# One 512-column product for the high and low activations in the residual's dense layers and in the second block's gate and up

## What is computed

```python
x = x + gate_f * ((jax.nn.silu(u_gate) * u_val) @ w_down[l])            # first block: down
...
for layer in range(DEPTH_2):
    h = h + hybrid_mixer(...)                    # ends in y @ w_mix_out: mixout0, mixout1
    h = h + memory_cross_attention(...)          # ends in o @ w_xo:      xo0, xo1
    hn = rmsnorm(h, norm_ffn_g[layer])
    if layer % 2 == 0:
        h = h + (jax.nn.silu(hn @ w_gate) * (hn @ w_up)) @ w_down       # up2, down2
    else:
        h = h + moe_swiglu(...)
```

## Time and profile before

| | |
|---|---|
| median of 3 executions | 2247.67 us (2243.60 to 2249.77) |
| the profiled execution | 2247.01 us, span 2245.3 us |
| TensorE matmul, busy | 2183.2 us, 97% of the span |
| VectorE busy | 1701.4 us, 76% |
| ScalarE busy | 1296.6 us, 58% |
| DMA | 563.82 MB, mean 251 GB/s |
| granted TensorE clock, mean | 0.990 |

### The profile page before, as it was taken

How to read it: one execution, slowest core, us unless ns; L and a number is a source line. 1 busy time by engine, 2 the same in 40 slices (tenths; PEclk the granted TensorE clock), 3 DMA queues, 4 the chain that set the end, 5 groups by cost and what they waited for, 6 DMA issues and landing times.

```text
span 2245.3 us, 34129 instructions
## 1 busy us (share of the span) xinstructions
PE 2183.2 (97%) x13631; PEld 1948.4 (87%) x13631; DVE 1701.4 (76%) x1889; ACT 1296.6 (58%) x1289; POOL 76.1 (3%) x159
## 2 busy tenths in 40 slices
PE   7999999999999999999999999999999999999997
PEld 5989988999989899999898888888887888888886
DVE  6768967884785465558654888888888888888887
ACT  3564434763425444443344777777777777777775
POOL 5002200000000000000000000000000000000000
PEclk9999999999999999999999999999999999999999
DMA  9746858655635366555372799999999999999995
GB/s 287 193 127 217 269 175 236 175 173 178 175 116 173 104 170 177 181 155 156 116 239 81 268 365 361 369 329 365 359 369 350 321 370 362 364 345 358 365 365 184
DMA packets 414601, 563.82 MB, mean 251 GB/s; under 512 B 17098, under 2 KB 268212, under 8 KB 414448
## 3 DMA queue, kind: packets, MB, share of 16 engines
q1 hardware_dynamic: 409680, 555.26, 73.5%
q0 software_dynamic: 4768, 6.36, 1.2%
HBM read 559.75 MB, written 1.84 MB: 250 GB/s over the span
## 4 chain that ended last, share of the span: by engine, by line
PE 83%; DVE 8%; ACT 2%; issue 1%; DVEq 0%; ACTq 0%
PE pair L1174 59%; PE misc L1174 13%; PE pair L1234 4%; DVE wlo L1808 2%; DVE opf L1876 2%; PE misc L1717 1%; DVE wlo L2157 1%; PE pair L1685 1%; ACT whi L674 1%; PE misc L1274 1%; PE misc L1253 0%; DVE hl L1827 0%; PE misc L1694 0%; PE misc L1695 0%; PE misc L1365 0%
## 5 line engine op out<-in xcount | busy, mean ns | idle before, releaser
L2157 DVE TENSOR_TENSOR wlo<-raw,whi 128x2048 fp32r<-128x2048 f32 x336 | 764.2, 2290 | 119.6 <-ACT whi L1056 118.9
L1056 ACT CAST whi<-raw 128x2048 fp32r<-128x2048 f32 x336 | 643.1, 1917 | 205.0 <-PE pair L1174 123.5
L1808 DVE TENSOR_TENSOR wlo<-raw,whi 128x2048 fp32r<-128x2048 f32 (+2 forms) x158 | 348.5, 2209 | 157.9 <-ACT whi L674 157.2
L1174 PE MATMUL pair<-hh,whi 128*128 128x256 f32 x1408 | 405.5, 288 | 8.4 <-DVE opl L1827 4.1
L1174 PE MATMUL pair<-hl,whi 128*128 128x256 f32 x1408 | 400.7, 285 | 0.0
L1174 PE MATMUL pair<-hh,wlo 128*128 128x256 f32 x1408 | 400.4, 284 | 0.0
L1174 PE MATMUL pair<-whi,oph 128*128 128x512 f32 x896 | 353.5, 395 | 5.2 <-issue 4.5
L1174 PE MATMUL pair<-wlo,oph 128*128 128x512 f32 x896 | 350.0, 391 | 0.0
L1174 PE MATMUL pair<-whi,opl 128*128 128x512 f32 x896 | 349.7, 390 | 0.0
L674 ACT CAST whi<-raw 128x2048 fp32r<-128x2048 f32 (+2 forms) x158 | 290.1, 1837 | 84.7 <-PE pair L1174 66.8
L1174 PE MATMUL pair<-oph,whi 128*128 128x256 f32 x976 | 279.4, 286 | 5.2 <-issue 3.0
(11 more groups left out here) (464 smaller groups left out, 2788.1 us busy)
## 6 DMA issues: line engine op xcount, KB each, us to landing
raw<-in_moe_w_gate_dram SPq DMA_DIRECT2D x112, 1024.0 KB, 7.1
raw<-in_moe_w_up_dram SPq DMA_DIRECT2D x112, 1024.0 KB, 7.3
raw<-in_moe_w_down_dram SPq DMA_DIRECT2D x112, 1024.0 KB, 7.0
raw<-in_w_in_dram SPq DMA_DIRECT2D x38, 1024.0 KB, 6.1
raw<-in_w_mod_dram SPq DMA_DIRECT2D x24, 1024.0 KB, 5.7
raw<-in_w_up_dram SPq DMA_DIRECT2D x44, 512.0 KB, 5.2
raw<-in_w_xkv_dram SPq DMA_DIRECT2D x16, 1024.0 KB, 5.7
raw<-in_ffn_w_gate_dram SPq DMA_DIRECT2D x22, 512.0 KB, 4.1
```

Source lines behind the costliest of these rows:

```text
L1056: act.copy(whi[:, q, :], raw[:, r, :]).then_inc(sem("hi_ready"), 1)
L1174: ins = pe.matmul(out_, lhs, rhs, start=start and i == 0, stop=stop and i == 2)
L1808: dve.tensor_tensor(wlo[:, i_ % SPLIT, 0:size], raw[:, raw_of(n), 0:size], whi[:, i_ % SPLIT, 0:size].bitcast(F32), ALU.subtract).then_inc ...
L2157: dve.tensor_tensor(wlo[:, q, :], raw[:, r, :], whi[:, q, :].bitcast(F32), ALU.subtract).then_inc(sem("lo_ready"), 1)
```

## The change

For six stages, listed in `TWO_SUMS`, the two products with the same high weights become one matmul. `hh` and `hl` (and `oph` and `opl`) are now two halves of one tensor `hx` (`opx`), so that a chunk's high and low part can be the moving operand together: 2 x 256 = 512 columns, in two runs. It fills a whole PSUM bank: high x high in columns 0 to 255, high x low in columns 256 to 511. The product of the low weights is added to the first half. The readers now add the second half as well.

```diff
+TWO_SUMS = ("down", "mixout0", "mixout1", "xo0", "up2", "down2")
...
-        hh = sb("hh", [P, DC, T], F32R)
-        hl = sb("hl", [P, DC, T], F32R)
+        hx = sb("hx", [P, 2, DC, T], F32R)
+        hh, hl = hx[:, 0], hx[:, 1]
...
+        up_sum = aview(3072, 3, 2, T)
...
+                            if groups[ups2[j]][0] in TWO_SUMS:
+                                act.wait_ge(sem("slot_used"), split_no[first_slot[ups2[j]]] + 1)
+                                act.copy(up_sum[:, j % 3], pair[:, pair_seq[ups2[j]] % PAIRS, :, T:2 * T]).then_inc(sem("up2_second"), 1)
                             act.wait_ge(sem("up2_gate"), j + 1)
                             act.activation(sg[:, j % 3], gate_n[:, j % 3], ACT.Silu).then_inc(sem("up2_silu"), 1)
...
+            def both(out_, w_hi, w_lo, x, start, stop):
+
+                pe.matmul(out_.rearrange("p (k t) -> p k t", k=2), w_hi, x, start=start, stop=False)
+                return pe.matmul(out_[:, 0:T], w_lo, x[:, 0], start=False, stop=stop)
...
-                            ins = three(pair[:, q, m, 0:T], wh[:, col], wl[:, col], operand(xh, x), operand(xl, x), start, stop)
+                            parts = operand(x_parts, x)
+                            if groups[g][0] in TWO_SUMS:
+                                ins = both(pair[:, q, m, :], wh[:, col], wl[:, col], parts, start, stop)
+                            else:
+                                ins = three(pair[:, q, m, 0:T], wh[:, col], wl[:, col], parts[:, 0], parts[:, 1], start, stop)
...
+            def second(g):
+
+                return pair[:, pair_seq[g] % PAIRS, :, T:2 * T]
+
             def add_modulated(g, j, gate):
                 ps = group(g)
+                if groups[g][0] in TWO_SUMS:
+                    for m in range(2):
+                        t = 2 * j + m
+                        ins = dve.scalar_tensor_tensor(xT[:, t], second(g)[:, m], mod[:, gate + t:gate + t + 1], xT[:, t], ALU.mult, ALU.add)
+                    link(ins)
...
             def add_plain(g, j):
                 ps = group(g)
+                if groups[g][0] in TWO_SUMS:
+                    link(dve.tensor_tensor(xT[:, 2 * j:2 * j + 2, :], second(g), xT[:, 2 * j:2 * j + 2, :], ALU.add))
                 dve.tensor_tensor(xT[:, 2 * j:2 * j + 2, :], ps, xT[:, 2 * j:2 * j + 2, :], ALU.add).then_inc(sem("dve_read"), 1)
...
-                            dve.tensor_tensor(gate_n[:, j % 3], ps[:, 0], rt[:], ALU.mult).then_inc(sem("up2_gate"), 1)
+                            if groups[ups2[j]][0] in TWO_SUMS:
+                                dve.wait_ge(sem("up2_second"), j + 1)
+                                both = up_sum[:, j % 3]
+                                link(dve.tensor_tensor(both, ps, both, ALU.add))
+                            else:
+                                both = ps
+                            dve.tensor_tensor(gate_n[:, j % 3], both[:, 0], rt[:], ALU.mult).then_inc(sem("up2_gate"), 1)
...
-                            dve.tensor_tensor(uf[:, j % 3], ps[:, 1], sg[:, j % 3], ALU.mult).then_inc(sem("dve_read"), 1)
+                            dve.tensor_tensor(uf[:, j % 3], both[:, 1], sg[:, j % 3], ALU.mult).then_inc(sem("dve_read"), 1)
                     for j, g in enumerate(stage_groups["down2"]):
                         ps = group(g)
-                        link(dve.tensor_tensor(down_n, ps, rt[:].unsqueeze(1).to_broadcast([P, 2, T]), ALU.mult))
+                        by_token = rt[:].unsqueeze(1).to_broadcast([P, 2, T])
+                        link(dve.tensor_tensor(down_n, second(g), by_token, ALU.mult))
+                        link(dve.tensor_tensor(xT[:, 2 * j:2 * j + 2, :], down_n, xT[:, 2 * j:2 * j + 2, :], ALU.add))
+                        link(dve.tensor_tensor(down_n, ps, by_token, ALU.mult))
                         dve.tensor_tensor(xT[:, 2 * j:2 * j + 2, :], down_n, xT[:, 2 * j:2 * j + 2, :], ALU.add)\
                             .then_inc(sem("dve_read"), 1)
```

More of the change, by code:

```diff
@@ L402, in build_program, with up2_parts @@
         fin = [b[:, 16:24, :] for b in (oph, opl)]
+        xin_at, fin_at = opx[:, :, 0:8, :], opx[:, :, 16:24, :]
+        up_sum = aview(3072, 3, 2, T)
+        def up2_parts(j):
+            return opx[:, :, j] if j < 16 else hx[:, :, j - 16]
         def up2_out(k, j):
-            return (oph, opl)[k][:, j] if j < 16 else (hh, hl)[k][:, j - 16]
+            return up2_parts(j)[:, k]
         values_at = [b[:, 16:24, :].rearrange("p a b -> p (a b)").rearrange("p (i d) -> p i d", i=TB) for b in (oph, opl)]
@@ L1187, in free_pair, with dense_group @@
                     pe.wait_ge(sem(f"{groups[before][2]}_read"), reads_at[before])
+            def both(out_, w_hi, w_lo, x, start, stop):
+                pe.matmul(out_.rearrange("p (k t) -> p k t", k=2), w_hi, x, start=start, stop=False)
+                return pe.matmul(out_[:, 0:T], w_lo, x[:, 0], start=False, stop=stop)
             def operand(x, c):
-                return x(c) if callable(x) else x[:, c]
-            def dense_group(g, xh, xl, weights_move=False, width=256, chunk0=0, each_chunk=None):
+                return x(c) if callable(x) else x[:, :, c]
+            def dense_group(g, x_parts, weights_move=False, width=256, chunk0=0, each_chunk=None):
                 free_pair(g)
@@ L1213, in dense_group @@
                             tok = slice(m * P, (m + 1) * P)
-                            ins = three(pair[:, q, m, 0:width], wh[:, 0:width], wl[:, 0:width], xh[:, x, tok],
-                                        xl[:, x, tok], start, stop, True)
+                            ins = three(pair[:, q, m, 0:width], wh[:, 0:width], wl[:, 0:width], x_parts[:, 0, x, tok],
+                                        x_parts[:, 1, x, tok], start, stop, True)
                         else:
                             col = slice(m * P, (m + 1) * P)
-                            ins = three(pair[:, q, m, 0:T], wh[:, col], wl[:, col], operand(xh, x), operand(xl, x), start, stop)
+                            parts = operand(x_parts, x)
[3 more added lines that the diff above has]
+                                ins = three(pair[:, q, m, 0:T], wh[:, col], wl[:, col], parts[:, 0], parts[:, 1], start, stop)
                     ins.then_inc(sem("slot_used"), 1)
@@ L1276, in sums, with into_norm @@
                     ins.then_inc(sem("squares_summed"), 1)
-            def into_norm(stage, name, xh, xl, beside=None, **how):
+            def into_norm(stage, name, x_parts, beside=None, **how):
                 each = how.pop("each_chunk", None)
                 for j, g in enumerate(stage_groups[stage]):
-                    dense_group(g, xh, xl, each_chunk=each if j == 0 else None, **how)
+                    dense_group(g, x_parts, each_chunk=each if j == 0 else None, **how)
                     if j >= 1:
@@ L1375, in _ @@
                     qk_squares(i - 1)
-            dense_group(stage_groups["va"][0], hh, hl, weights_move=True, width=P)
+            dense_group(stage_groups["va"][0], hx, weights_move=True, width=P)
             qk_squares(6)
@@ L1483, in _ @@
             pe.wait_ge(sem("mem_ready"), DC)
-            into_norm("down", "mix0", oph, opl, beside=stage_groups["xk0"][0], each_chunk=lambda c: (sem("u_lo"), c + 1))
+            into_norm("down", "mix0", opx, beside=stage_groups["xk0"][0], each_chunk=lambda c: (sem("u_lo"), c + 1))
             for l in range(2):
@@ L1491, in _ @@
                     for g in stage_groups[f"{stage}{l}"]:
-                        dense_group(g, hh, hl, each_chunk=h_chunk(k0) if first else None)
+                        dense_group(g, hx, each_chunk=h_chunk(k0) if first else None)
                         first = False
@@ L1609, in _ @@
                 if l == 0:
-                    into_norm("xo0", "ffn0", hh, hl, each_chunk=lambda c: (sem("xo_lo"), c // 2 + 1))
+                    into_norm("xo0", "ffn0", hx, each_chunk=lambda c: (sem("xo_lo"), c // 2 + 1))
                     for i, g in enumerate(stage_groups["up2"]):
-                        dense_group(g, *fin, each_chunk=h_chunk(NORM["ffn0"]) if i == 0 else None)
+                        dense_group(g, fin_at, each_chunk=h_chunk(NORM["ffn0"]) if i == 0 else None)
                         if i == 0:
@@ L1618, in _ @@
                     pe.wait_ge(sem("mem_ready"), 2 * DC)
-                    into_norm("down2", "mix1", lambda c: up2_out(0, c), lambda c: up2_out(1, c), beside=stage_groups["xk1"][0],
+                    into_norm("down2", "mix1", up2_parts, beside=stage_groups["xk1"][0],
                               each_chunk=lambda c: (sem("u2_lo"), c + 1))
```

32 lines of the change are left out of this document (16 added, 16 removed).

## The result

The changed kernel takes 2263.69 us (median of 4 runs, 2258.38 to 2269.86) against 2247.81 us for the one before beside it: a ratio of 1.0068, 95% interval 1.0054 to 1.0082, 15 us slower. The forecast was 2253 us, with 2261 as its upper end. The profiled execution took 2258.38 us with a span of 2256.7; it is the shortest of the four.

A forecast was written before the change was run, and what follows sets the result against it. TensorE was taken as the bound, with VectorE's and ScalarE's loop becoming it in up2. Terms 5.6 + 2.9 - 2.0 - 0.9 = +5.6 us on the profiled 2247.0 gave 2252.6, forecast 2253 us, range 2243 to 2261.

The forecast's parts named there:

- the price of the wait in `mixout`: First xq group of each layer: TensorE waits 2.3 us for chunk 6, +1.45 us each, +2.9 in all.
- up2: VectorE's addition inside the loop makes a turn 6.00 us against TensorE's 5.55; with the earlier start, +5.6 us.
- down2 and xo0: down2 gains 2.3 us, its end costs 1.45, net -0.9; xo0 and group 0 end 1.07 earlier, counted in up2's +5.6.
- down: 176 merged triples gain 2.3 us; of 0.9 us added at the stage's end 0.6 is hidden: -2.0 us.
- The added reads at `down2`'s end: Two linked operations lengthen down2's end by 1.45 us, with no slack before the root, so all goes through.
- The pair: One product of 512 and one of 256 columns take 346.7 ns instead of 360.0, 13.3 ns less per triple.
- The experts: The experts behind the second block are untouched and must keep their length; otherwise none of this is the cause.
- A: TensorE stays the bound in up2 at turns of 5.55 us: -9.5 us, 2238 us; 8%, and 3% with the mixout waits.
- B: The 512-column product with its operand in two runs takes 240 ns and gains nothing: +13.1, 2261 us; 9%.
- C: The wait in mixout doesn't arise: +1.0, 2249 us; 8%.
- D: ScalarE's copy of 0.59 us is not hidden in up2's turn: +12 more, 2265 us; 4%.
- E: A product left out gives back only 2.6 ns, not 13.3: +11.7, 2259 us; 3%.

The follow-up runs named there:

- e5: Changed kernel with five products put into TensorE's stream ahead of the wait for chunk 6 in both layers' first xq group: 2255.84 us, 1.0046 to the kernel before.
- e8: Changed kernel with VectorE's low weights made behind the gate in up2 and behind the addition in both mixout and xo stages: 2240.31 us, 0.9971 to the kernel before.
- e11: The kernel with two sums in all six stages and the new order in all loops, run a second time: 2238.90 us, 0.9955 to the kernel before.
- e1: The changed kernel run again, unchanged: 2265.05 us, 1.0070 to the kernel before.
- e4: The change in down, xo0 and down2 only, against the kernel before: 2245.22 us, 0.9982.
- e12: The kernel before the change, unchanged, for a second profiled execution: 2248.18 us, 0.9998.
- e6: Changed kernel without VectorE's addition in up2, ScalarE's copy still made: 2253.23 us, 1.0033 to the kernel before.
- `up2` alone: The change in up2 only, against the kernel before, run twice: 2257.58 us, 1.0039, and 2256.14 us, 1.0040.
- `mixout` alone: The change in mixout0 and mixout1 only, against the kernel before: 2256.67 us, 1.0039.
- e10: Kernel before the change, three products everywhere, with only VectorE's low weights moved behind the gate or addition: 2247.83 us, 1.0002.

## Why the prediction was wrong

**The step that failed** is the price of the wait in `mixout`: "TensorE waits 2.3 us and has gained 0.85: **+1.45 us each**, +2.9". Its mechanism and size were right: additions every 6.91 us (forecast 6.92), chunk 6 at 725.17 - 696.30 = 28.87 us (28.8), a wait of 2.38. But the step let TensorE go on at 2.4 GHz behind it, and had no term for the clock at all. The four pieces around `mixout` sum to 115.0 to 116.5 us in the six executions with three products there, and to 122.9 to 129.5, 127.6 in the mean, in the six that have the unfilled wait: +11.6 us instead of +2.9. e5 shows what part of it the idle TensorE causes: with five products in the wait, which give nothing, the sum falls to 120.1 and the run by 5.4 us. The Trainium skill ("TensorE: Matmul & The Clock Gate", Part 1: The HAM clock gate) says that the clock is set by how busy TensorE was of late. The traces agree as far as the wait goes: it was followed by 6.8 to 13.7 us at the low clock in all twelve places, against at most 6.8 in e5, e8 and e11, where it is filled or gone, and 3.4 in the kernel before. But in e1 the clock stayed low from 728.6 to 742.2, through the 32 one-column sums and into the 144 products, while TensorE was busy without a gap; what of that work kept it low is not shown. The table shows, too, that the kernel before already lost clock at this place in layer 1 of its first profile (b' is 18.89, b 17.39), and that the prediction passed over.

**The other terms.** *up2* was right: turns of 5.94 (forecast 6.00) and 6.66, 121.4 us from gate 0 to gate 20 (810.47 to 931.90; forecast 122.5). With `xo0` and `down2`, c grew by 4.5 to 5.1, in traces that all have the low clock behind `down2`; forecast 5.6 - 0.9 = 4.7. *down2 and xo0* gave 2.0 us on TensorE in e4 (241.40 against 243.37), where 0.85 + 2.3 were forecast, and the added reads took 1.4 of it back: -0.6, against -0.9 - 0.85. (e4's c is lower by 2.06 because it lacks the low clock, 1.5 us.) *down* gave -1.1 us, forecast -2.0: the root's start is 0.76 us earlier than before (565.37 against 566.13) in an execution that ran 0.38 later ahead of the stage (transposes on TensorE at 415.40 against 415.02), and e4 and e11 give the same -1.1. The gain of its four groups was 1.45 us instead of 2.3, since three of them run at 353.3 ns; the end cost 0.3 as forecast. The added reads at `down2`'s end went through as said. The load follows the last addition and the square, and the root follows it, in the chain of the kernel after:

```profile
999.45 0.70 DVE xT L2384
1000.18 0.63 ACT work L703
1000.83 1.28 ACT L705
1002.12 0.48 ACT rt L705
```

*The pair* was 346.7 ns as forecast in some groups and 353.3 in others, half the saving. On the path that took 1.5 us of the forecast 7.5 in the first trace of the changed kernel (three groups in `down`, three in `xo0`, one in `down2`), 2.1 in e1, and nothing where the loop is the bound. *The experts* kept their length: from the end of (b') to the end of the program it is 1069.2 us after and 1069.3 before (1066.9 in e1, 1071.3 in e12).

**The sum** with the measured terms is 11.6 + 4.8 (c) - 1.1 (`down`) = +15.3 us against the 15.4 to 15.9 of the medians. That it comes so close is luck in part: the 11.6 is a mean over kernels whose single traces give 6.9 to 13.5.

**The rivals.** A is out: the loop is the bound. What it would have given shows in e8 and e11, where both loops are loosened: 7 and 8 us faster by the medians, against A's 9.5. B is out: it needs 360 ns a pair, and no group had over 353.7. C is out by the wait in all six traces. D is out: the copy is hidden (e6). E is out: a product less gave 6.7 or 13.3 ns, not 2.6. By the rule of the Trainium skill ("TensorE: Matmul & The Clock Gate", Back-to-back issue gap) it would be 2.5; here the measurement differs and decides.

**What stays open:** why a group of pairs takes one price or the other; how long the clock stays low behind a wait, 6.8 us or twice that; and some 2 us by which the medians of `up2` alone (8.0 and 7.7) lie above its 5.7, twice measured and not located (3.5 to 3.8, if the low clock behind `down2`, which three traces without pairs have and both of `up2` alone lack, goes with the kernel and not with the execution; that is not shown). As `mixout` alone measured 8.8 us against 12.0 in its trace (128.0 - 116.0), single traces and medians differ by some 3 us here either way.

## What to carry to other kernels

A wait of TensorE is priced with what runs behind it: look up the granted clock there, above all where the next work is thin (one-column sums). When two engines hand over in turns, ask of an added instruction whether it stands in the loop. Here the same addition cost 10 us between `wlo` and the gate, and nothing once `wlo` was made behind the gate; that order, worth nothing in the kernel before (e10), together with the one in `mixout`, turned 15 us slower into 8 us faster (e11). And before two stretches of two traces are compared, look whether the clock was the same in both: here one stretch of 3.4 us at the low clock, present in one and missing in the other, was worth 1.5 us, as much as the terms in question.

## What was not expected of the hardware

The granted clock was 0.50 for 13.6 us in which TensorE was busy without a gap (e1), after a wait of 2.4 us, part of 12 products and 32 one-column products; with the wait filled it did not fall in layer 1 at all. And pairs of products of 512 and 256 columns ran at 346.7 or 353.3 ns at a granted clock of 1.00, one price for a whole group: the same pattern over the groups of `down`, `xo0` and `mixout` in all nine traces, while in `up2` the same code ran at either. Products of 256 columns alone stood at 119.9 to 120.0 ns in all eight stretches of the kernel before that I read.
